# A two-block transformer kernel on one core: five changes to the order of work around its tile stream

## The reference

```
mod = silu(c) @ ada_w + ada_b                  # 6 vectors of 2048: shifts, scales, gates (also for ctx)
z   = modulate(rmsnorm(x)) @ w_in              # q, k, v of attention; r, k, v, lora inputs of the recurrence
attn = windowed attention with sinks over z and the context's k, v
kk  = normalized(k * k_k) per head of 64 features;   decay, a = from small "lora" products
S   = S * w + (S @ -kk) (kk * a)^T + v k^T     # recurrence over context, then tokens, both directions
x  += g1 * (concat(attn, rw) @ w_out)
x  += g2 * ((silu(h @ w1) * (h @ w3)) @ w2)    # h = modulate(rmsnorm(x)); d_ff = 5632
x   = rmsnorm(x, final_norm_g)
# second block
q, k, v, gate_r, mq, gate_m = rmsnorm(x, norm_a) @ w_in_a
x  += concat(retention(rotary(q), rotary(k), v) normalized * silu(gate_r), memory branch) @ w_out_a
x  += concat(dilated attention, memory branch) @ w_out_b
out = rmsnorm(x, final_norm_g_2)
```

## Time and profile before

| | |
|---|---|
| median of 3 runs | 3832.03 us (3831.39 to 3832.28) |
| the profiled execution | 3829.78 us |
| its span, first to last instruction | 3827.8 us |
| PE busy | 3666.6 us, 96% |
| DVE, ACT, POOL busy | 1924.7, 1652.3, 1390.9 us |
| mean granted PE clock | 0.985 |
| moved by DMA | 668.91 MB, mean 175 GB/s |

### The profile page before, as it was taken

One profiled execution on the slowest core, in us unless ns is written; L12 is line 12 of the kernel. 1 busy time (PEld: TensorE's weight loads), 2 busy tenths in 40 slices (PEclk: granted clock), 3 DMA queues, 4 the chain that ended last, 5 costly groups with the idle time before them and its releaser, 6 DMA issues.

```text
span 3827.8 us, 72287 instructions
## 1 busy us (share of the span) xinstructions
PE 3666.6 (96%) x30708; PEld 3191.5 (83%) x30708; DVE 1924.7 (50%) x2454; ACT 1652.3 (43%) x2132; POOL 1390.9 (36%) x631
## 2 busy tenths in 40 slices
PE   8999989889988999999999999999999999999998
PEld 5777878777778888888878888888888888888887
DVE  3248877556555883443445444335344334433333
ACT  3442226544444443444445444435444444444443
POOL 2332223000023454554534454534444433443443
PEclk9999999999999999999999999999999999999999
DMA  8876774000025776565555555445655555555553
GB/s 299 299 273 228 280 275 156 27 4 4 15 75 185 238 264 193 185 195 185 189 162 167 181 168 178 160 160 170 205 177 175 175 175 173 174 175 175 174 171 124
DMA packets 183375, 668.91 MB, mean 175 GB/s; under 512 B 20464, under 2 KB 20464, under 8 KB 182416
## 3 DMA queue, kind: packets, MB, share of 16 engines
q1 hardware_dynamic: 176688, 643.12, 50.6%
q10 hardware_dynamic: 5088, 16.98, 1.3%
q0 software_dynamic: 1280, 4.20, 0.3%
HBM read 655.82 MB, written 8.39 MB: 174 GB/s over the span
## 4 chain that ended last, share of the span: by engine, by line
PE 80%; DVE 9%; ACT 4%; issue 2%; DMA 2%; PEld 1%; POOL 1%; ACTq 0%; SPq 0%; PEldq 0%; DVEq 0%; POOLq 0%
PE ps L1083 67%; DVE whl L2113 2%; ACT whl L1593 2%; DVE raw L2197 1%; PEld ps L1083 1%; PE ps L1337 1%; DMA raw<-in_mem 1%; PE ps L1323 1%; POOL whl L2726 1%; PE ps L1314 1%; PE ps L1581 1%; PE ps L1565 1%; ACT work L1593 1%; PE ps L1008 1%; PE ps L1246 1%
## 5 line engine op out<-in xcount | busy, mean ns | idle before, releaser
L1083 PE MATMUL ps<-halves,whl 128*128 128x256 f32 (+1 forms) x14752 | 2575.9, 335 | 71.5 <-DVE halves L2113 23.6
L1083 PEld LDWEIGHTS ps<-halves,whl 128*128 128x128 f32 x14752 | 2238.0, 190 | 375.8 <-issue 76.6
L2726 POOL TENSOR_TENSOR whl<-raw,whl 128x1024 fp32r<-128x1024 f32 x508 | 1261.2, 2483 | 1773.5 <-ACT whl L1593 1773.2
L1593 ACT ACTIVATE whl<-raw 128x1024 fp32r<-128x1024 f32 x1016 | 1058.1, 1053 | 963.1 <-PE ps L1083 684.7
L2113 DVE TENSOR_TENSOR whl<-raw,whl 128x1024 fp32r<-128x1024 f32 x508 | 790.7, 1557 | 1136.1 <-ACT whl L1593 1135.9
L1083 PE MATMUL ps<-whl,halves 128*128 128x256 f32 x2752 | 485.6, 336 | 3.7 <-ACT whl L1593 3.4
L1083 PEld LDWEIGHTS ps<-whl,halves 128*128 128x128 f32 x2752 | 418.5, 189 | 60.9 <-ACT whl L1593 4.2
L1593 ACT ACTIVATE work<-ps 128x512 f32<-128x512 f32 (+1 forms) x206 | 117.6, 575 | 286.2 <-PE ps L1083 229.9
L2197 DVE SCALAR_TENSOR_TENSOR raw<-raw,mix 128x1024 f32<-128x1024 f32 x128 | 235.8, 1869 | 3.5 <-DMA raw<-in_adaT 3.3
L2726 POOL TENSOR_TENSOR halves<-mix,halves 128x256 fp32r<-128x256 f32 (+1 forms) x15 | 25.0, 1685 | 408.9 <-ACT halves L1593 408.9
L2113 DVE TENSOR_TENSOR work<-work,ps 128x512 f32<-128x512 f32 x155 | 106.2, 685 | 108.6 <-ACT work L1593 107.5
(11 more groups left out here) (266 smaller groups left out, 2372.6 us busy)
## 6 DMA issues: line engine op xcount, KB each, us to landing
raw<-in_ffn SPq DMA_DIRECT2D x264, 512.0 KB, 4.3
raw<-in_w_kv SPq DMA_DIRECT2D x192, 512.0 KB, 3.6
raw<-in_w_in_b SPq DMA_DIRECT2D x160, 512.0 KB, 3.5
raw<-in_adaT SPq DMA_DIRECT2D x128, 512.0 KB, 5.4
raw<-in_w_in_a SPq DMA_DIRECT2D x128, 512.0 KB, 3.6
raw<-in_ada SPq DMA_DIRECT2D x64, 512.0 KB, 5.8
raw<-in_mem SPq DMA_DIRECT2D x64, 512.0 KB, 5.1
raw<-in_w_out_a SPq DMA_DIRECT2D x48, 512.0 KB, 3.5
```

Of the source, the lines that this page charges most:

```text
L1083: p = self.e.matmul(o, x, y, start=bi not in begun, stop=final and kc == 3 and m == len(pairs) - 1, skip_group_check=True)
L1593: return self.e.activation(out, in_, func, **kw)
L2726: return self.e.tensor_tensor(out, a, b, op)
```

## The change

1. **Begin of the recurrence.** The steps of dense (d), attention (t), key norms (n), lora (l), key scales (s) and the first seven steps of `prepare(0)` (p) are put in one written series, `HEAD`. The fences at the recurrence's begin are gone. The constant loads are issued by SP. The key scales use transposes in two other banks, and buffers are moved; in their place stand waits for the last tiles of `w_gd`.
2. **Its written series.** `FIRST_ORDER` and all of `ORDER` are other strings of the same steps (two steps of the output's work go from the last string to the end).
3. **Gate tiles beside the down projection.** `BESIDE_FFN` becomes `(1, 0, 0, 0)`, and the other 14 `adaT` tiles follow one after each tile of `ffn2` 0 to 3. `ev_x` waits only for the modulation columns that it uses.
4. **Roots behind retention's products.** `HA` gets x times gain, without the root, as x is finished; the first two tiles of products come ahead of the root's chain. The root is multiplied in later: into the rotary tables, into the gates, and as a factor per token in the scores.
5. **Splits without fences.** `project` has no fence; the split of group 3 is chained to the heads (`last_mix`), and each split waits for the last product from its own buffer alone.

```
-BESIDE_FFN = (1, 0)
+BESIDE_FFN = (1, 0, 0, 0)
+BESIDE_SUM = 4
...
         for n in range(8):
-            add("ffn2", [n], range(k0, k1))
+            for kg in range(k0, k1):
+                names += [("ffn2", n, kg), *itertools.islice(modulation, int(k0 == 0 and n < BESIDE_SUM))]
...
-        run_all((dense, 1), (limited(attention, 20), 1), (self.key_norms(), 1))
-        self.rwkv_lora()
-        scales = self.key_scales()
-        run_all((attention, 1), (limited(scales, 6), 3))
-        self.rwkv_load()
-        rest(scales)
-        self.rwkv()
+        self.rwkv_begin()
+        preps = [self.prepare(n) for n in range(8)]
+        in_order(HEAD, d=chain(dense, (0,)), t=attention, n=self.key_norms(), l=self.rwkv_lora(), s=self.key_scales(), p=limited(preps[0], PREPARED))
+        self.bonus_constants()
+        self.rwkv(preps)
...
-        self.root_of_sums(4)
-        self.f4 = self.fence()
-        self.begin_retention()
...
-    def rwkv(self):
-        self.f0 = self.fence()
-        self.rwkv_begin()
-        self.fr = self.fence()
-        preps = [self.prepare(n) for n in range(8)]
+    def rwkv(self, preps):
...
+    def behind_sums(self, made):
+
+        products = alternate(*made[2:4])
+        rest(limited(products, 2))
+        self.root_of_sums(4)
+        self.f4 = self.fence()
+        self.begin_retention()
+        for g in made[:2]:
+            rest(g)
+        rest(products)
+        self.root_of_tokens()
...
-        run_all((heads, 1), (mixed, 2), (chain(*[limited(g, 5) for g in jobs[:4]]), beside))
-        self.f9 = self.fence()
-        if which:
-            self.reload_x2()
-        self.mix_done(name, 3)
+        run_all((chain(heads, self.last_mix(name)), 1), (mixed, 2), (chain(*[limited(g, 5) for g in jobs[:4]]), beside))
         for g in jobs:
             rest(g)
+
+    def last_mix(self, name):
+        self.mix_done(name, 3)
+        if name == "w_out_b":
+            self.reload_x2()
+        yield
...
# PE, key_scales
-                m = self.e.matmul(self.G(c % 2)[:, 128 * b:128 * b + 128], squares[:, c, 128 * b:128 * b + 128], self.ident, start=True, stop=True)
+                m = self.e.transpose(self.G(2 + c % 2)[:, 128 * b:128 * b + 128], squares[:, c % 4, 128 * b:128 * b + 128], self.ident)
...
# ACT, ev_x
+        if r == 4:
+            if n == 0:
+                self.wait_ge("gain_v", "both")
+                self.wait_ge("mm", self.used["HA"])
+            for c in (2 * n, 2 * n + 1):
+                self.act(self.acts["HA"][0][:, c, :], self.xt[:, c, :], ACT.Copy, scale=self.gs[:, 16 + c:17 + c]).then_inc(self.sig("n_hi", (4, c)), 1)
...
# DVE, key_scales
         for c in range(8):
+            self.wait_ge("mm", TILES[GATE - 4 + c // 2].n)
             self.wait_ge("kk_mm", ("in", c))
...
# DVE, finish_on of a gated tile
+            if job.key[0] == "w_in_a":
+                self.wait_ge("rms_v", 5)
+                self.tt(g, g, self.rst[1].unsqueeze(1).to_broadcast([128, 2, 256]), MUL).then_inc(self.sig("ev_v", (job.key, "r")), 1)
...
# SP
+    def rwkv_load(self):
+        self.wait_ge("mod_v", LATE - 1)
+        self.e.dma_start(self.A("aup"), self.io["a_up"]).then_inc(self.sig("ld_rwkv", 0, 16), 16)
+        self.wait_ge("at_v", (15, "mask"))
+        self.wait_ge("rope_v", (9, "add"))
+        self.e.dma_start(self.A("rwc"), self.io["rwkv_c"]).then_inc(self.sig("ld_rwkv", 1, 16), 16)
+        self.wait_ge("mm", TILES[GATE - 3].n)
+        for i, (dst, name) in enumerate((("wup", "w_up"), ("w0r", "w0"))):
+            self.e.dma_start(self.A(dst), self.io[name]).then_inc(self.sig("ld_rwkv", i + 2, 16), 16)
...
-FIRST_ORDER = "iipipiipiipipppipiiiiiiiiippiiiipiiiiiiiiii"
+HEAD = "ddtnltndlntndldltdnlttndtnltddtdntndtndntdddtstdsttsdsdtstdstsdtpptspptppp"
+PREPARED = HEAD.count("p")
+FIRST_ORDER = "iipipiiippipiiippiiiiiipiipipipiiiiiiiiiiii"
```

More of the change, by code:

```diff
@@ L421, in schedule @@
             for n in range(8):
-                rest(self.gemm("ffn2", n, range(k0, k1), self.halved("B", "HB"), "v2",
-                               lambda j, n=n, part=part: self.ev_x(j, n, 5, 4 if part == 2 else None), kbase=k0))
-        self.root_of_sums(4)
-        self.f4 = self.fence()
-        self.begin_retention()
+                sums = self.gemm("ffn2", n, range(k0, k1), self.halved("B", "HB"), "v2",
+                                 lambda j, n=n, part=part: self.ev_x(j, n, 5, 4 if part == 2 else None), kbase=k0)
+                rest(self.after(sums, modulation, (int(part == 0 and n < BESIDE_SUM),)))
         self.m2, self.heads_begun, self.ring, self.ring_name = 0, 0, self.w2, "w"
-        heads = self.pipeline(self.memory_groups(0, "w_in_a", 24) + self.retention_groups(), 3, self.normed(4, 5, "HA"), self.norm_in_place(0, 4))
-        self.project("w_out_a", 0, 6, heads, 3)
+        heads = self.pipeline(self.memory_groups(0, "w_in_a", 24) + self.retention_groups(), 3, None, self.norm_in_place(0, 4))
+        self.project("w_out_a", 6, heads, 3)
         self.root_of_sums(6)
@@ L435, in schedule @@
         heads = self.pipeline_tight(self.dilated_groups(), last)
[L436 removed]
+        self.project("w_out_b", 7, heads, 2)
         self.root_of_sums(7)
@@ L790, in key_norms @@
     def key_norms(self):
-        yield from range(10)
+        yield from range(11)
     def key_scales(self):
@@ L797, in out_mean, with rwkv_lora @@
         yield from range(4)
-    rwkv_lora = rwkv_load = rwkv_begin = split_mix = nothing
+    rwkv_begin = split_mix = bonus_constants = nothing
+    def rwkv_lora(self):
+        yield from range(6)
     out_rest = no_steps
@@ L861, in pipeline @@
             if heads is None:
-                for _, g in made[:2]:
-                    rest(g)
-                self.beside(normed, made[2][1], made[3][1])
+                if normed:
+                    for _, g in made[:2]:
+                        rest(g)
+                    self.beside(normed, made[2][1], made[3][1])
+                else:
+                    self.behind_sums([g for _, g in made])
             elif ratio == MEMORY_TURNS:
@@ L942, in dilated_groups, with dil_head, project @@
         return res
-    mem_head = ret_head = dil_head = no_steps
-    def project(self, name, which, r, heads, beside):
+    mem_head = ret_head = no_steps
+    def dil_head(self, *a):
+        yield from range(5)
+    def project(self, name, r, heads, beside):
         outs = [(0, 256 * fb, "B", 128 * fb, "wide", 0) for fb in range(2)]
@@ L1167, in key_norms @@
             yield
-        yield
+        yield from range(2)
     def key_scales(self):
@@ L1475, in ev_x, with root_of_tokens @@
             self.sums = (r, n)
+        if r == 4:
+            for c in (2 * n, 2 * n + 1):
+                self.ready["HA", c] = ("n_lo_v", (4, c))
     def root_of_sums(self, r):
         self.add_squares()
+    def root_of_tokens(self):
+        self.bank(5, "mh_s", "roots")
+        self.wait_ge("rms_v", 5)
+        for tb in range(2):
+            m = self.e.matmul(self.X(1)[:, 2 * tb:2 * tb + 2], self.rst[1][:, 128 * tb:128 * tb + 128], self.ident[:, 0:2], start=True, stop=True)
+        m.then_inc(self.sig("sum_mm", "roots"), 1)
     def swiglu(self, job, j, pos):
@@ L2045, in mem_head @@
         self.wait_ge("mh_mm", (h, "s"))
-        self.act(p[:, 0:512], self.X(0), ACT.Copy).then_inc(self.sig("mh_s", (h, "p")), 1)
+        if h < 4:
+            self.wait_ge("mh_s", "roots")
+            for qb in range(2):
+                at = slice(256 * qb, 256 * qb + 256)
+                self.act(p[:, at], self.X(0)[:, at], ACT.Copy, scale=self.cols[:, 6 + qb:7 + qb]).then_inc(self.sig("mh_s", (h, "p") if qb else (h, "p", 0)), 1)
+        else:
+            self.act(p[:, 0:512], self.X(0), ACT.Copy).then_inc(self.sig("mh_s", (h, "p")), 1)
         k = 8 * (h % 8)
@@ L2556, in ev_x @@
         if gate is not None:
-            self.wait_ge("mod_v", 23 if gate == 2 else 47)
+            self.wait_ge("mod_v", 8 * gate + n)
         if job.wide:
```

153 lines of the change are left out of this document (98 added, 55 removed).

## The result

The changed kernel takes 3803.44 us (3793.95 to 3805.91, 4 runs) against 3832.16 (3831.39 to 3834.72, 4 runs) for the one before: a ratio of 0.9915, interval [0.9903, 0.9927]. Two more comparisons, made beside the experiments, gave 3800.60 (0.9919 [0.9898, 0.9939]) and 3796.95 (0.9918 [0.9904, 0.9931]). So, by the medians of each comparison, it is faster by 29 to 34 us; the forecast was 31. The ratios are the recorded ones and not quotients of the medians, which would be 0.9925 in the first comparison. The profiled execution took 3803.8 us.

What follows compares the result with a forecast made beforehand. PE bounds the kernel, busy 3666.6 of 3827.8 us, so reordering can remove 161 us idle plus lost clock. Terms 11 + 2 + 3 + 11 + 4 = 31 us give 3801, forecast range 3792 to 3811, 8-in-10 range 3788 to 3818.

Steps and rivals of the forecast that it cites:

- Part 1: Begin of the recurrence: 41.05 us becomes about 28.1, less 2 us for new waits; gain 11, bounds 4 and 16.
- bound of 16: Begin of the recurrence, better end of the gain: no new waits, and the lost clock comes back.
- The recurrence's idle moves from 38 us by more than 10: Sign that the prediction is wrong: PE's idle time in the recurrence changes by over 10 us either way.
- lower bound of 4: Begin of the recurrence, worse end of the gain: each of four waits costs 2 us more, 12.9 - 2 - 8, rounded up.
- Part 2: Written series in the recurrence: same steps in another order, small gain of 2 us; at most 10 gained or 6 lost.
- which an order can't mend: Recurrence: PE's 3.2 us wait at line 1323 for nothing shown, left out of the bound of the series' gain.
- Part 3: Gate tiles: 7 us gained beside `ffn1` and `ffn3`, 4 lost beside `ffn2`, net 3; bounds +7 and -4.
- Part 4: Start of retention: 40.7 us becomes 28.3 with a new 2 us wait; gain taken as 11, bounds 6 and 13.
- Part 5: Output projections: `w_out_a`'s 2.03 us wait goes, `w_out_b`'s 4.08 becomes 1.9; gain 4, bounds 2 and 5.
- half given back: Rival, whole kernel: stalls move to new waits, gain 16 us, 3816 (3811 to 3822); chance 0.18.
- the series was not worse: Rival, recurrence: the new order adds idle, 36 us in all, giving 3835; chance 0.04.
- All of it and the clock: Rival, whole kernel: every part three quarters toward its better end, about 42 us, 3790 (3782 to 3792); chance 0.12.

Runs made afterwards that it cites:

- part 1 alone: The changed kernel with the other four parts undone, but for the shorter wait of `ev_x`: 3825.19 us, ratio 0.9988 to the kernel before.
- run 8: The changed kernel with each of the 384 transposes of the inversion issued twice, the second writing the same result: 3820.09 us in one whole run.

## Why the prediction was right

The sum was 31 us, and three of its five terms came true by the waits that they named. The two terms of the begin and the series are right only taken together, and that is in part luck. Stage by stage, the mean of three profiles of the changed kernel is 33.7 us below that of two of before: A +1.4, B -17.6, R +1.5, means -0.3, F -5.1, S -9.9, W -3.1, retention and dilated part +1.0, D -1.6. By its terms:

- **Part 1: 11 forecast, about 12 by these two stages, by two errors that cancel; 1 to 8 by the whole time of part 1 alone.** B lost 18.1 us (179.3 in eleven runs, 197.4 in two). The tail of 22.5 was forecast at 24; the last dense product ended at 722.61 instead of 716.94, 4.2 of which lie ahead in A, so the dense stretch grew by 1.4 us and not 4.2, since the scales fell into what had been idle; the new waits for DVE's `w_gd` tiles, charged at 2, don't show, so the bound of 16 was passed. What was missing is the other side: R is longer by 6 us with the new begin and old strings (364.2 against 358.4, two profiles each), where the issue gaps grow from 9 to 16 us and 1 us is busier PE. The sum had no term for it. "The recurrence's idle moves from 38 us by more than 10" did not happen, 39.7, and hid this. The lower bound of 4 should have been 3 by its own figures (12.9 - 2 - 8 is 2.9).
- **Part 2: 2 forecast.** 2 us at the same clock, 6 in the plain means (364.2 and 358.4), with a spread of 353 to 364 for one code, so its size isn't shown. The forecast had no mechanism either: "Nothing in the trace prices an order". The bound, "which an order can't mend", was right in a way that I had not seen: each of line 1323's three gaps, 3.2 us for nothing shown, ended 1.4 to 1.5 us after a packet of instructions had landed.
- **Part 3: 3 forecast, 4.0 measured.** Beside `ffn1` and `ffn3` idle fell by 6.5 us (7 forecast). Beside `ffn2` 2.5 were lost where 4 stood: the loads ran at 334 GB/s, over the 323 that I took for the limit. That they are what is short there fits ACT's waits, 23.5 of 47 us for `raw` tiles.
- **Part 4: 11 forecast, 10.0 measured.** The new wait came in the sixth tile as computed, 2.38 us for 2; the sum left out the slower clock behind it, 1.5 us in five of eight profiles.
- **Part 5: 4 forecast, 5.3 measured** (W 3.4, D 1.9). `w_out_b`'s wait is 1.98 for 1.9, and the reload was late by up to 1.8 for "a us". W gave 1.4 us more than the 2.03 of its wait, time in which PE is shown busy; the sum had no such term.

Of the rivals, half given back asked for waits in part 1 that don't show; the series was not worse. "All of it and the clock" stood at 3790 with a gain of about 42, though three quarters of the way to each better end add up to 46, 3786. 3790 is where a single run came (3791.8 us, the third profile, clock 0.988), not the medians.

## What to carry to other kernels

When a stall is taken away ahead of a stretch of very short matmuls, look whether the waits in that stretch turn into waits "for nothing": add both kinds up before you count a gain. Where a fence stands in a queue, put the work that feeds the bound engine in front of the wait, not behind it. With parts worth 2 to 10 us in a run that scatters by 8, compare stages between like instructions in several profiles of each kernel; one pair of profiles had blamed the step series for 5.7 us that no later run put on it. And compare at like granted clocks: for one code it alone moved a stage by 8 us.

## What the runs showed of the hardware

- PE stops in long runs of short products and goes on 1.2 to 1.6 us after a packet of the instruction queue has landed; in the recurrence such gaps were 8 to 18 us in sum. That the gaps are the fetching is concluded from this coincidence, in all 266 gaps of fourteen profiles where chance would give one in ten, and fits their fall in run 8. Changing the fetching itself wasn't tried.
- PE's clock makes more difference between runs of one kernel than three of the five parts: with the granted clock of the recurrence at 0.96 the stage took 364.3 us, at 0.99 353.1, with the same instructions (PE busy 324.6 and 316.1, so 8.5 of the 11.2 us).
- After a wait of 2.38 us 48 products took 10.13 us, without it half of 17.20: a short wait can cost more than its length, here 1.5 us. It isn't sure to, even in one code: after this wait the changed kernel's clock was 0.83 in two profiles and 1.00 in the third, and after the wait of 1.98 us at `w_out_b` 1.00 in two and 0.77 in the third. After the longer wait of 4.08 us there, in the kernels with fences, it was 0.78 to 0.80 in all four.
- When POOL's and DVE's splits overlapped at the start of retention, two took 5.66 and 5.83 us, where one alone takes 2.40 and 1.22.
